# Alternating row halves in the small products, 32 bytes in front of the working memory, and a varied order of split matmuls in sixteen projections

## The chip, the core and the metric

The kernel runs on one core of a Trainium2 chip. A core has TensorE (PE, with its weight loads shown apart as PEld), VectorE (DVE), ScalarE (ACT), GpSimd (POOL) and SyncE (SP), which issues most DMAs. The metric is the device time of one execution in microseconds, lower is better. The kernel before takes 2512.82 us (median of three runs, 2508.73 to 2514.59).

## The reference

One layer of a hybrid decoder trunk over 256 tokens of width 2048, all in float32. The part that the change touches is the input projection and the RWKV-7 branch.

```python
def hybrid_mixer(h, positions, w_in, ...):
    z = h @ w_in
    z_sc, z_rw, z_ret, z_nsa, z_gate = _split(z, GROUP_SIZES)
    o_a = short_conv_mixer(*_split(z_sc, SC_SIZES), sc_conv)
    o_b = rwkv7_mixer(z_rw, ...)
    o_c = retention_mixer(*_split(z_ret, RET_SIZES), positions)
    o_d = nsa_mixer(*_split(z_nsa, NSA_SIZES), positions, ...)
    merged = g_a * (o_a @ w_a) + g_b * (o_b @ w_b) + g_c * (o_c @ w_c) + g_d * (o_d @ w_d)
    return merged @ w_out

def wkv7_scan(r, w, k, v, kk, a):          # inside rwkv7_mixer: 8 heads of 64 channels
    def step(state, inp):
        r_t, w_t, k_t, v_t, kk_t, a_t = inp
        sa = jnp.einsum('bhvk,bhk->bhv', state, -kk_t)
        state = (state * w_t[:, :, None, :]
                 + sa[..., None] * (kk_t * a_t)[:, :, None, :]
                 + v_t[..., None] * k_t[:, :, None, :])
        return state, jnp.einsum('bhvk,bhk->bhv', state, r_t)
    _, y = lax.scan(step, s0, xs)

def reference(...):
    x = x + rms_norm(hybrid_mixer(rms_norm(x, ...), ...), ...)
    x = x + rms_norm(memory_cross_attention(rms_norm(x, ...), rms_norm(mem, ...), ...), ...)
    x = x + rms_norm(conv_ffn(rms_norm(x, ...), ...), ...)
```

## The kernel before

Each engine runs a program of its own, written out by hand; semaphores alone tie them together. No scheduler moves anything: on each engine the instructions run as the code lists them.

**The stages.** First the normed input is made (until about 28 us). Then come the 79 tiles of the list `MIX`: one 1 MB weight tile each, multiplied with the 256 tokens, with the work of the four mixers laid between them by the table `steps`. From about 772 us the weights stream: gates and branches, output projection, cross-attention, and the feed-forward part up to the end. SP loads the weights of `MIX` into a ring of four slots.

**Two ways to multiply.** `project` (line 396) multiplies in plain float32. A plain float32 product shows as two records in the trace, each with its weight load, so that 16 products make 32 records. The first sixteen projections, `project_split` (lines 414 and 417), and the whole streaming part (`half`, lines 797 and 800) use a split form instead: a value is held as a rounded "high" part and a "low" rest. One product of 512 columns takes the high weights times the high and low activations side by side (`high`), and one of 256 columns the low weights times the high activations (`cross`); both go to one PSUM bank of 512 columns. Such a product is one record. ACT makes the high parts, DVE the low ones. The semaphore `hsplit_low` tells that a quarter of the activations is split; projection 0 waits for each quarter when it comes to it.

**The small products.** The RWKV-7 branch holds two heads of 64 channels in the two halves of the 128 partitions. Its products are 64 x 64 (some 64 x 128), read one half of the partitions and write the same half of PSUM, in the banks of `sm`. `per_head` (products at line 452) runs 32 of them: 16 for the lower half, then 16 for the upper half, each to a place of its own: eight 64-wide products fill a bank. It is called by `rw_s1` and `rw_s2` (128 wide), `rw_s3`, `rw_s4`, `rw_level` and `rw_level2` (64 wide). `four` (products at line 531) runs four products, or four sums of two or three, for each half in the same manner, for the four chunks `rw_chunk_a`, `rw_chunk_b`, `rw_chunk_c`. One projection lies between one such group and the next, while DVE or ACT evacuates the group's result and makes the operands of the next.

**The memory.** SBUF tensors are laid one behind another: the constants `cst`, the vectors `vec` (552 columns, 2208 bytes a partition), and `region`, in which all working tensors are placed by offset. `region` begins at byte 25632, which is 32 above a multiple of 64.

Of the kernel before, what the change touches and what calls it, by code (L numbers as in the profile page):

```python
# [19 lines left out]
T = 256  # L20
P = 128
# [84 lines left out]
NVEC = sum(c for _, c in VEC)  # L106
# [33 lines left out]
def program(nc, A, const_dram, decay_dram, const_at, out):  # L140
# [4 lines left out]
    with ctx:  # L145
        def sb(name, shape, dt=f32):
            return ctx.enter_context(nc.sbuf_tensor(name, shape, dt))
# [3 lines left out]
        def sem(name):  # L151
            if name not in sems:
                sems[name] = ctx.enter_context(nc.semaphore(name))
            return sems[name]

        NC = const_dram.shape[1]
        cst = sb("cst", [P, NC])
        vec = sb("vec", [P, NVEC])

        region_at = nc.sbuf_base  # L160
        sb("region", [P, REGION])
# [4 lines left out]
        def part(a, *dims, dt=f32):  # L166

            placed[0] += 1
            t = nc.alloc_sbuf_tensor_at(f"part{placed[0]}", [P, math.prod(dims)], dt, offset=region_at + 4 * a)
            names = "abcdef"[:len(dims)]  # L170
            return t[:, :].rearrange(f"p ({' '.join(names)}) -> p {' '.join(names)}", **dict(zip(names, dims)))

        def partr(a, *dims):

            return part(a, *dims, dt=mybir.dt.float32r)
# [20 lines left out]
        def vv(name, i=0, n=1, rows=P):  # L196
            a, _ = VEC_AT[name]
            return vec[0:rows, a + i:a + i + n]
# [8 lines left out]
        sm = ctx.enter_context(nc.psum_tensor("sm", [P, 6, 512], f32))  # L207
# [19 lines left out]
        hsplit = partr(A0 + 8208, KT, 2 * T)  # L227
# [48 lines left out]
        cross = part(21504, 2, T)  # L276
# [105 lines left out]
        def _(pe):  # L382
# [17 lines left out]
            def project_split(n):  # L400

                if n >= 2:
                    pe.wait_ge(outd, n - 1)
                b = bank[:, n % 2, :]
                for h in range(2):
                    pe.wait_ge(sem("early_low"), 2 * n + h + 1)
                    w = wearly[(2 * n + h) % 4]
                    for k in range(8):
                        if n == 0 and k % 4 == 0:
                            pe.wait_ge(sem("hsplit_low"), 2 * h + k // 4 + 1)  # L410
                        x, last = hsplit[:, 8 * h + k, :], h == 1 and k == 7
                        for term in ("cross", "high") if last else ("high", "cross"):
                            if term == "high":
                                mm = pe.matmul(b, w[:, 0, k, :], x, start=h == 0 and k == 0, stop=last,  # L414
                                               skip_group_check=True)
                            else:
                                mm = pe.matmul(b[:, T:2 * T], w[:, 1, k, :], x[:, 0:T], start=False, stop=False,  # L417
                                               skip_group_check=True)
                    mm.then_inc(sem("early_used"), 1)
                pe.sem_inc(used, 1)  # L420

# [16 lines left out]
            def per_head(fn):  # L438


                for h in range(2):
                    for g in range(16):
                        mm = fn(slice(64 * h, 64 * h + 64), g)
                return mm

            def b64(base, g, w=64):
# [42 lines left out]
            def rw_s1():  # L489
                pe.wait_ge(sem("rw_operands"), 1)  # L490
                pe.wait_ge(sem("rw_bonus_out"), 1)
                per_head(lambda r, g: small_mm(0, r, g, G["B"][r, g], QR[r, g, :, :], w=128)) \
                    .then_inc(sem("rw_s1_mm"), 1)

            def rw_s2():
                pe.wait_ge(sem("rw_s1_out"), 1)
                per_head(lambda r, g: small_mm(0, r, g, G["C"][r, g], QR[r, g, :, :], w=128)) \
                    .then_inc(sem("rw_s2_mm"), 1)

            def rw_s3():  # L500
                pe.wait_ge(sem("rw_s2_out"), 1)
                per_head(lambda r, g: small_mm(0, r, g, QR[r, g, 0, :], G["B"][r, g])).then_inc(sem("rw_s3_mm"), 1)
                per_head(lambda r, g: small_mm(2, r, g, G["Vc"][r, g], eye(r))).then_inc(sem("rw_s3_mm"), 1)
# [19 lines left out]
                        .then_inc(sem("rw_p2_mm"), 1)  # L523

            def four(base, off, fn):
                for h in range(2):
                    r = slice(64 * h, 64 * h + 64)
                    for i in range(4):
                        pairs = fn(r, i)
                        for q, (a, b) in enumerate(pairs):  # L530
                            mm = pe.matmul(sm[r, base + i // 2, off + i % 2 * 64:off + i % 2 * 64 + 64], a, b,  # L531
                                           start=q == 0, stop=q == len(pairs) - 1)
                return mm

            v4 = lambda a: a.rearrange("p (i t) -> p i t", t=64)
# [2 lines left out]
            def rw_chunk_a(c):  # L538

                if c == 0:  # L540
                    pe.wait_ge(sem("rw_x_ready"), 6)
                else:
                    pe.wait_ge(sem("rw_state"), c)
                    pe.wait_ge(sem("rw_y_out"), c)
                four(0, 0, lambda r, i: ([(QR[r, 4 * i + c, 0, :], S4[r, i])] if c else [])
                     + [(G["L2"][r, 4 * i + c], G["V"][r, 4 * i + c])]).then_inc(sem("rw_rhs_mm"), 1)

            def rw_chunk_b(c):

                pe.wait_ge(sem("rw_rhs_out"), c + 1)  # L550
                four(2, 0, lambda r, i: [(G["X"][r, 4 * i + c], X04[r, i])]).then_inc(sem("rw_u_mm"), 1)

            def rw_chunk_c(c):

                pe.wait_ge(sem("rw_u_out"), c + 1)
                if c < NCH - 1:
                    four(2, 128, lambda r, i: [(G["Bt"][r, 4 * i + c], U4[r, i]),
                                               (G["Ct"][r, 4 * i + c], G["V"][r, 4 * i + c])]) \
                        .then_inc(sem("rw_ds_mm"), 1)
                four(0, 128, lambda r, i: ([(S4[r, i], QR[r, 4 * i + c, 1, :])] if c else [])  # L560
                     + [(U4[r, i], G["M1"][r, 4 * i + c]), (G["V"][r, 4 * i + c], G["M2"][r, 4 * i + c])]) \
                    .then_inc(sem("rw_y_mm"), 1)
# [206 lines left out]
            for n, (what, i) in enumerate(MIX):  # L769
                for s in steps.get((what, i), []):  # L770
                    s()
                if n < EARLY:
                    project_split(n)
                elif what == "gate":
                    project(n, M=24)
                elif what == "cmp":
                    nsa_cmp_hidden(i)
                elif what == "rv":
                    take(n)
                    project_tokens(n, hT, big[:, n % 2, :])  # L780
                else:
                    project(n)
# [151 lines left out]
            with pe.Fori(0, 8) as i:  # L934
                for t in range(2):
                    pe.wait_ge(prod_out, i * 2 + (R_DOWN + t - 1))
                    for j in range(4):
                        if t == 0:
                            pe.wait_ge(sem("g_split"), 11 * j + 11)
                        for h, n in ((0, 8), (1, 3)):  # L940
                            k = 11 * j + 8 * h

                            x, k0 = (gA, k) if k < 8 else (gB, k - 8)
# [6 lines left out]
        def _(act):  # L950
            used, outd = sem("chunk_used"), sem("chunk_out")
            act.sem_inc(sem("prod_out"), 2)
            act.dma_start(cst[:, :], const_dram).then_inc(sem("consts_loaded"), 16)
            act.dma_start(vec[:, :], A["vec"]).then_inc(sem("consts_loaded"), 16)
            cp, idt = ACT.Copy, ACT.Identity

            def std(k):
# [312 lines left out]
            for j in range(KT):  # L1270
# [9 lines left out]
                elif 8 <= j < 12:  # L1280
                    q = j - 8
# [3 lines left out]
            for j in range(KT):  # L1285
# [3 lines left out]
                elif 2 <= j < 6:  # L1289
                    q = j - 2  # L1290
# [5 lines left out]
                elif 11 <= j < 15:  # L1296
                    q = j - 11
# [52 lines left out]
            for q in range(4):  # L1350
                act.wait_ge(sem("res_ready"), 4 + q + 1)
                for k in range(4 * q, 4 * q + 4):
                    mm = act.activation(yT[:, k, :], res[:, k, :], cp, scale=vv("ln_ffn_pre", k))
# [7 lines left out]
            for first, count, g in ((0, 8 // PAIR_STEP, gA), (4, (FT - 8) // PAIR_STEP, gB)):  # L1361
                with act.Fori(0, count) as i:
# [6 lines left out]
                    for p in range(PAIR_STEP):  # L1369
                        for s in range(2):  # L1370
                            j = 2 * p + s
                            m = M_UP + 4 * first + j
                            at = lambda k, v: i * (2 * PAIR_STEP * k) + v
# [776 lines left out]
```

## Time and profile before

| what | before |
|---|---|
| median of three timed runs | 2512.82 us |
| their range | 2508.73 to 2514.59 us |
| span of the profiled execution, first to last instruction | 2503.8 us |
| median of the runs less this span | 9.0 us |
| PE busy | 2398.1 us, 96% |
| weight loads on PE busy | 2085.0 us, 83% |
| DVE busy | 1384.9 us, 55% |
| ACT busy | 1045.6 us, 42% |
| POOL busy | 236.1 us, 9% |
| mean granted clock of PE | 0.975 of full speed |

The span comes from one profiled execution, and the last 9.0 us of a timed run lie around it. "Busy" counts a stretch once even where records overlap, so a group's busy time can be far less than its count times its mean duration. The granted clock is 1.00 where PE runs at 2.4 GHz and 0.50 where it runs at 1.2 GHz. A row of the timeline merges records of one kind that follow each other: its second number is the time from the first start to the last end.

### The profile page before, as it was taken

The numbers are of one execution on the slowest core, as the hardware profiler recorded it, in microseconds if no ns is written. First come the engines' busy times: TensorE is split into PE (matmuls) and PEld (weight loads), VectorE is DVE, ScalarE is ACT, GpSimd is POOL, SyncE is SP. The second block draws the span as 40 slices with busy tenths as digits, with TensorE's granted clock in tenths as the row PEclk, the third lists the DMA queues.
The fourth block names the chain that finished last, engine by engine and source line by source line (L and its number), as shares of the span: only waits on it lengthen the run. The fifth ranks groups of instructions, "written<-read, shape, count | busy, mean of one in ns | idle before, by whom it ended". The sixth has DMA issues, their size and how long they took to land.

```text
span 2503.8 us, 38637 instructions
## 1 busy us (share of the span) xinstructions
PE 2398.1 (96%) x14320; PEld 2085.0 (83%) x14320; DVE 1384.9 (55%) x1676; ACT 1045.6 (42%) x1463; POOL 236.1 (9%) x240
## 2 busy tenths in 40 slices
PE   5989999999999999999999999896999999999996
PEld 4869989789888888887887888785888888888885
DVE  5661110221118666666677544356877777776665
ACT  4320001112114555555444444345655555555553
POOL 0120100000000000000421000031111111111110
PEclk9989997999999999999999999998999999999998
DMA  6512222233334555556555554252655555555663
GB/s 224 185 51 85 98 102 78 97 133 113 124 118 152 185 187 186 189 189 212 194 171 165 181 173 153 93 188 86 198 186 186 184 182 188 189 163 188 186 185 127
DMA packets 104459, 392.77 MB, mean 157 GB/s; under 512 B 11600, under 2 KB 20048, under 8 KB 94000
## 3 DMA queue, kind: packets, MB, share of 16 engines
q1 hardware_dynamic: 104080, 390.31, 47.2%
q8 instruction: 67, 1.10, 0.2%
q10 hardware_dynamic: 288, 1.17, 0.1%
q14 instruction: 24, 0.20, 0.0%
HBM read 389.34 MB, written 2.10 MB: 156 GB/s over the span
## 4 chain that ended last, share of the span: by engine, by line
PE 73%; issue 18%; DVE 6%; ACT 1%; POOL 1%; DMA 0%; DVEq 0%; POOLq 0%; ACTq 0%
PE bank L797 29%; PE bank L800 15%; PE bank L396 13%; PE sm L452 3%; PE bank L414 2%; PE bank L426 2%; PE sm L531 1%; PE bank L417 1%; PE bank L615 1%; DVE part L1876 1%; DVE part L1970 1%; DVE part L1539 1%; PE sm L905 1%; PE sm L435 1%; PE sm L887 1%
## 5 line engine op out<-in xcount | busy, mean ns | idle before, releaser
L797 PE MATMUL bank<-part,part 128*128 128x512 f32 x4224 | 1488.4, 399 | 35.1 <-issue 16.3
L800 PE MATMUL bank<-part,part 128*128 128x256 f32 x4224 | 1150.6, 282 | 0.0
L1876 DVE TENSOR_TENSOR part<-part,part 128x1024 fp32r<-128x1024 f32 (+1 forms) x632 | 795.0, 1268 | 370.7 <-ACT part L1139 358.4
L797 PEld LDWEIGHTS bank<-part,part 128*128 128x128 f32 x4224 | 783.8, 189 | 212.0 <-issue 20.1
L800 PEld LDWEIGHTS bank<-part,part 128*128 128x128 f32 x4224 | 799.7, 189 | 21.5
L1139 ACT ACTIVATE part<-part 128x1024 fp32r<-128x1024 f32 (+1 forms) x632 | 662.8, 1050 | 349.7 <-PE bank L800 320.9
L396 PE MATMUL bank<-part,part 128*128 128x256 f32 (+1 forms) x1632 | 364.3, 383 | 0.0
L396 PEld LDWEIGHTS bank<-part,part 128*128 128x128 f32 (+1 forms) x1632 | 307.4, 190 | 50.0 <-issue 5.1
L1213 ACT ACTIVATE part<-bank 128x256 f32<-128x256 f32 x236 | 90.3, 382 | 291.1 <-PE bank L797 291.1
L992 ACT ACTIVATE part<-bank 128x256 f32<-128x256 f32 (+1 forms) x59 | 22.7, 384 | 413.3 <-PE bank L396 375.5
L1884 DVE TENSOR_TENSOR part<-bank,part 128x256 f32<-128x256 f32 (+1 forms) x236 | 99.8, 423 | 132.9 <-ACT part L1213 132.8
L1476 POOL TENSOR_TENSOR part<-part 128x256 f32 (+1 forms) x48 | 48.1, 1003 | 763.2 <-DVE part L1884 763.2
L797 PE MATMUL sm<-part,part 128*128 128x512 f32 x320 | 110.8, 397 | 1.3 <-DVE part L1890 0.7
L414 PE MATMUL bank<-part,part 128*128 128x512 f32 x256 | 90.9, 403 | 8.7 <-DVE part L1575 8.7
L800 PE MATMUL sm<-part,part 128*128 128x256 f32 x320 | 79.4, 281 | 0.0
L452 PEld LDWEIGHTS sm<-part 64*64 64x64 f32 x1088 | 71.6, 139 | 7.6 <-issue 7.6
L452 PE MATMUL sm<-part 64*64 64x64 f32 (+1 forms) x1088 | 73.7, 233 | 2.1 <-DVE part L1639 2.1
L1501 POOL TENSOR_TENSOR part<-part 128x256 f32<-128x256 f32 x44 | 32.5, 738 | 424.1 <-DVE part L2051 424.1
L417 PE MATMUL bank<-part,part 128*128 128x256 f32 x256 | 69.8, 283 | 0.0
L797 PEld LDWEIGHTS sm<-part,part 128*128 128x128 f32 x320 | 56.8, 188 | 11.0 <-DVE part L1890 1.5
L800 PEld LDWEIGHTS sm<-part,part 128*128 128x128 f32 x320 | 60.1, 188 | 5.8
L414 PEld LDWEIGHTS bank<-part,part 128*128 128x128 f32 x256 | 47.7, 190 | 20.4 <-issue 9.7
(304 smaller groups left out, 1576.0 us busy)
## 6 DMA issues: line engine op xcount, KB each, us to landing
part<-in_w_up SPq DMA_DIRECT2D x176, 512.0 KB, 4.5
part<-in_w_g SPq DMA_DIRECT2D x104, 512.0 KB, 4.2
part<-in_w_dn SPq DMA_DIRECT2D x64, 512.0 KB, 3.5
part<-in_w_out SPq DMA_DIRECT2D x32, 512.0 KB, 4.0
part<-in_w_mk SPq DMA_DIRECT2D x32, 512.0 KB, 4.3
part<-in_w_mv SPq DMA_DIRECT2D x32, 512.0 KB, 3.9
part<-in_w_q SPq DMA_DIRECT2D x32, 512.0 KB, 3.8
part<-in_w_o SPq DMA_DIRECT2D x32, 512.0 KB, 3.9
```

Of the source, the lines that this page charges most:

```text
L396: mm = pe.matmul(big[0:M, n % 2, 0:rhs_n], w[:, k * M:(k + 1) * M], x[:, k, :], start=k == 0, stop=k == KT - 1)
L414: mm = pe.matmul(b, w[:, 0, k, :], x, start=h == 0 and k == 0, stop=last, skip_group_check=True)
L417: mm = pe.matmul(b[:, T:2 * T], w[:, 1, k, :], x[:, 0:T], start=False, stop=False, skip_group_check=True)
L426: mm = pe.matmul(dst[:, s * P:(s + 1) * P], x[:, k, s * P:(s + 1) * P], ring[:, n % NSLOT, k, :], start=k == 0, stop=k == KT - 1)
L452: return pe.matmul(sm[rows, b, c:c + w], lhsT, rhs, start=start, stop=stop)
L797: mm = pe.matmul(dst, w[:, 0, k, :], x[:, k0 + k, :], start=start and k == 0, stop=last, skip_group_check=True)
L800: mm = pe.matmul(dst[:, T:2 * T], w[:, 1, k, :], x[:, k0 + k, 0:T], start=False, stop=False, skip_group_check=True)
L1139: act.activation(wsplit[(2 * m + h) % 4][:, 0, 0:n, :], raw[:, m % 2, h, 0:n, :], cp) .then_inc(sem("hi_done"), 1)
L1213: act.activation(cross[:, b, :], bank[:, b, T:2 * T], cp).then_inc(sem("cross_out"), 1)
L1476: pool.tensor_tensor(sq[:, n % 2:n % 2 + 1, :], tile, tile, MUL).then_inc(sem("y_sq"), 1)
L1876: tt(w[:, 1, 0:n, :], raw[:, m % 2, h, 0:n, :], w[:, 0, 0:n, :].bitcast(f32), SUB).then_inc(sem("lo_done"), 1)
L1884: tt(dst, bank[:, b:b + 1, 0:T], cross[:, b:b + 1, :], ADD).then_inc(sem("prod_out"), 1)
```

## The change

Three things are edited.

First, `per_head` and `four` issue for the lower and the upper half in turn, and the upper half is shifted by half of the places, so that the two neighbours write different PSUM banks. Second, `vec` gets 8 more columns that nothing reads: `region`, `rstd` and `small` move up by 32 bytes, and `region` then begins at byte 25664, a multiple of 64. Third, `project_split` varies the order of its products. The second half of each projection runs backwards. Projections 1, 5, 9 and 13 run eight `high` and then eight `cross` products. Projections 2, 6, 10 and 14 issue each `high` product as two of 256 columns with the same weights. For projection 0 the second half of the weights waits for the last quarter of the activations at once.

```diff
-        vec = sb("vec", [P, NVEC])
+        vec = sb("vec", [P, NVEC + 8])
@@ project_split
-                    for k in range(8):
-                        if n == 0 and k % 4 == 0:
-                            pe.wait_ge(sem("hsplit_low"), 2 * h + k // 4 + 1)
-                        x, last = hsplit[:, 8 * h + k, :], h == 1 and k == 7
-                        for term in ("cross", "high") if last else ("high", "cross"):
-                            if term == "high":
-                                mm = pe.matmul(b, w[:, 0, k, :], x, start=h == 0 and k == 0, stop=last,
-                                               skip_group_check=True)
-                            else:
-                                mm = pe.matmul(b[:, T:2 * T], w[:, 1, k, :], x[:, 0:T], start=False, stop=False,
-                                               skip_group_check=True)
+                    grouped, halves = n % 4 == 1, n % 4 == 2
+                    terms = [("high", k) for k in range(8)] + [("cross", k) for k in range(8)] if grouped else \
+                        [(term, k) for k in range(8) for term in ("high", "cross")]
+                    if h == 1:
+                        terms = terms[::-1]
+                    for at, (term, k) in enumerate(terms):
+                        if n == 0 and at % 8 == 0:
+                            pe.wait_ge(sem("hsplit_low"), 2 * h + at // 8 + 1 if h == 0 else 4)
+                        x, last = hsplit[:, 8 * h + k, :], h == 1 and at == 15
+                        first = h == 0 and at == 0
+                        if term == "cross":
+                            mm = pe.matmul(b[:, T:2 * T], w[:, 1, k, :], x[:, 0:T], start=False, stop=last,
+                                           skip_group_check=True)
+                        elif halves:
+                            pe.matmul(b[:, 0:T], w[:, 0, k, :], x[:, 0:T], start=first, stop=False,
+                                      skip_group_check=True)
+                            mm = pe.matmul(b[:, T:2 * T], w[:, 0, k, :], x[:, T:2 * T], start=False, stop=last,
+                                           skip_group_check=True)
+                        else:
+                            mm = pe.matmul(b, w[:, 0, k, :], x, start=first, stop=last, skip_group_check=True)
@@ per_head
-                for h in range(2):
-                    for g in range(16):
-                        mm = fn(slice(64 * h, 64 * h + 64), g)
+                for g in range(16):
+                    for h in range(2):
+                        mm = fn(slice(64 * h, 64 * h + 64), (g + 8 * h) % 16)
@@ four
-                for h in range(2):
-                    r = slice(64 * h, 64 * h + 64)
-                    for i in range(4):
-                        pairs = fn(r, i)
-                        for q, (a, b) in enumerate(pairs):
-                            mm = pe.matmul(sm[r, base + i // 2, off + i % 2 * 64:off + i % 2 * 64 + 64], a, b,
-                                           start=q == 0, stop=q == len(pairs) - 1)
+                rows = [slice(64 * h, 64 * h + 64) for h in range(2)]
+                for i in range(4):
+                    at = [(i + 2 * h) % 4 for h in range(2)]
+                    pairs = [fn(rows[h], at[h]) for h in range(2)]
+                    for q in range(len(pairs[0])):
+                        for h in range(2):
+                            a, b = pairs[h][q]
+                            c = off + at[h] % 2 * 64
+                            mm = pe.matmul(sm[rows[h], base + at[h] // 2, c:c + 64], a, b,
+                                           start=q == 0, stop=q == len(pairs[h]) - 1)
@@ scalar
-            act.dma_start(vec[:, :], A["vec"]).then_inc(sem("consts_loaded"), 16)
+            act.dma_start(vec[:, 0:NVEC], A["vec"]).then_inc(sem("consts_loaded"), 16)
```

PE, projection 0, as its second half of the weights (`part_63`) begins; before, it reads:

```order
L417 MATMUL bank<-part_61,part_62 128x256
L414 MATMUL bank<-part_61,part_63 128x512 [waits hsplit_low,early_low]
L417 MATMUL bank<-part_61,part_63 128x256
L414 MATMUL bank<-part_61,part_63 128x512
L417 MATMUL bank<-part_61,part_63 128x256
```

PE at the same place in the changed kernel (line 414 has become 427, line 417 has become 419):

```order
L419 MATMUL bank<-part_61,part_62 128x256
L419 MATMUL bank<-part_61,part_63 128x256 [waits hsplit_low,early_low]
L427 MATMUL bank<-part_61,part_63 128x512
L419 MATMUL bank<-part_61,part_63 128x256
L427 MATMUL bank<-part_61,part_63 128x512
```

The half begins with a `cross` product, and its wait for `hsplit_low` is now for all four quarters and no longer for three.

PE in a projection with halved `high` products (lines 422 and 424), changed kernel, as one half of the weights ends and the next begins:

```order
L422 MATMUL bank<-part_61,part_62 128x256
L424 MATMUL bank<-part_61,part_62 128x256
L419 MATMUL bank<-part_61,part_62 128x256
L419 MATMUL bank<-part_61,part_63 128x256 [waits early_low]
L422 MATMUL bank<-part_61,part_63 128x256
```

Three products of 256 columns stand where one of 512 and one of 256 stood, which is 16 more products in each of the four projections. In `per_head` and `four` the number of products, their shapes and their waits stay; only which half each one works on changes, and the rows of such a list don't name the half. The lists of SP, DVE, ACT and POOL hold the same instructions in the same order.

## Rows read from the trace of the kernel before

**Rows 1.** The page: PE's busy time; costliest group, with count, busy us, mean ns.

```profile
PE 2398.1 (96%) x14320; PEld 2085.0 (83%) x14320; DVE 1384.9 (55%) x1676; ACT 1045.6 (42%) x1463; POOL 236.1 (9%) x240
...
L797 PE MATMUL bank<-part,part 128*128 128x512 f32 x4224 | 1488.4, 399 | 35.1 <-issue 16.3
```

**Rows 2.** Waits, 120 to 200 us: who waited for whom, us, times, longest.

```profile
PE sm L486 <- DVE part L1632: 7.6, 1, 7.6
...
PE sm L463 <- ACT part L996: 3.8, 1, 3.8
```

**Rows 3.** Windows: length, busy us and records by engine, granted clock, DMA share, GB/s.

```profile
175.00:180.00 5.00, 5.00 (x29) 5.00 (x29) 0.00 (x0) 0.00 (x0) 0.00 (x0) 0.50 0.01 3
...
200.00:250.00 50.00, 50.00 (x554) 45.65 (x553) 7.35 (x6) 3.58 (x6) 5.58 (x7) 1.00 0.23 85
```

**Rows 4.** Groups by shape on PE, 160 to 480 us: busy us, mean ns.

```profile
L452 PE MATMUL sm<-part 64*64 64x64 f32 x960 | 54.9, 220 | 0.0
L531 PE MATMUL sm<-part 64*64 64x64 f32 x448 | 31.4, 251 | 0.0
...
L452 PE MATMUL sm<-cst,part 64*64 64x64 f32 x192 | 10.9, 220 | 0.0
```

**Rows 5.** Timeline of PE, 200 to 210 us: start, length, engine, line, records.

```profile
208.00 0.27 PE L452 MATMUL sm<-cst,part 64*64 64x64 f32 x1
208.05 0.22 PE L452 MATMUL sm<-part 64*64 64x64 f32 x1
208.10 0.22 PE L452 MATMUL sm<-cst,part 64*64 64x64 f32 x1
208.11 0.22 PE L452 MATMUL sm<-part 64*64 64x64 f32 x1
208.16 0.22 PE L452 MATMUL sm<-cst,part 64*64 64x64 f32 x1
```

**Rows 6.** Timeline of PE, 170 to 480 us: groups of small products, one projection.

```profile
170.33 11.98 PE L452 MATMUL sm<-part 64*64 64x128 f32 x64 [2.10 <-DVE part L1639]
...
190.77 6.82 PE L452 MATMUL sm<-part 64*64 64x128 f32 x64
197.52 7.17 PE L396 MATMUL bank<-part,part 128*128 128x256 f32 x32
...
218.79 7.14 PE L452 MATMUL sm<-cst,part 64*64 64x64 f32 x128
...
232.96 3.76 PE L452 MATMUL sm<-part 64*64 64x64 f32 x64
...
356.16 0.96 PE L531 MATMUL sm<-part 64*64 64x64 f32 x16
...
371.07 5.99 PE L531 MATMUL sm<-part 64*64 64x64 f32 x64
...
387.07 1.90 PE L531 MATMUL sm<-part 64*64 64x64 f32 x32
...
400.48 7.70 PE L531 MATMUL sm<-part 64*64 64x64 f32 x80
...
435.31 4.34 PE L531 MATMUL sm<-part 64*64 64x64 f32 x80
...
469.68 2.83 PE L531 MATMUL sm<-part 64*64 64x64 f32 x48
```

**Rows 7.** Timeline of DVE and of PE, 32 to 37 us: the first projection.

```profile
32.74 2.36 DVE L1575 TENSOR_TENSOR part<-part,part 128x1024 fp32r<-128x1024 f32 x2
...
34.12 0.47 PE L414 MATMUL bank<-part,part 128*128 128x512 f32 x1 [1.10 <-DVE part L1575]
34.42 0.28 PE L417 MATMUL bank<-part,part 128*128 128x256 f32 x1
...
34.77 0.28 PE L417 MATMUL bank<-part,part 128*128 128x256 f32 x1
...
36.50 0.39 PE L417 MATMUL bank<-part,part 128*128 128x256 f32 x2
```

## The prediction, made before the changed kernel was run

> **What bounds the kernel now.** I read the page first: PE is busy in 96% of the span, and every other engine in 55% or less [rows 1]. So the question for each edit is what it does to PE's own time, and where PE waits for others. The chain of waits between 120 and 200 us shows where it does: 3.8 us for ACT, at the end of a chain from DVE, and 7.6 us for DVE, in the stretch that prepares the RWKV-7 operands [rows 2]. That chain starts when the sixteen early projections end, so whatever delays them delays everything. From 200 us on PE has no idle time: the window from 200 to 250 us has 50.00 us busy of 50.00, with DVE busy 7.35 us, ACT 3.58 and the DMAs at 23% [rows 3]. What PE saves there is saved at the end, as long as the engines between two groups keep up.
>
> Then the small products. The groups by shape show three large ones of 64-wide products, 54.9, 10.9 and 31.4 us busy [rows 4]; two groups of 128-wide ones add 11.98 and 6.82 us [rows 6]. That is 116 us in which a quarter of the array works at a time. The timeline gives their pace: 128 records in 7.14 us, 0.056 us each [rows 6]. The most telling rows stand where one call of `per_head` ends and another begins, at 208 us [rows 5]. There the end of the first call (upper half, `part`) and the start of the second (lower half, `cst`) run together: starts at 208.00, 208.05, 208.10, 208.11, 208.16. The `cst` records start 0.10 and then 0.06 us apart, the `part` records 0.05 to 0.06 apart, each at its usual pace. Two halves side by side don't slow each other. They overlap only for the last three records of the old half, at each change of half.
>
> **The small products in turn.** If every product has a neighbour in the other half, all records can run as these six do. The step of one half is then 7.14 us less a tail of 0.22, over 127 steps less the 9 that the three changes of half already hide: 0.0586 us. A group of n records takes about 0.10 (first step) + (n/2 - 2) x 0.0586 + 0.22 (tail). From [rows 6], with the number of such groups that the timeline has:
>
> - 128 records: 7.14 us become 3.95, saved 3.2. Six of them: 19.1 us.
> - 64 records: 3.76 become 2.08, saved 1.7. Six: 10.1 us.
> - `four`, full clock: 16 records 0.96 become 0.67 (five groups, 1.4 us saved); 32 records 1.90 become 1.14 (three, 2.3 us); 80 records 4.34 become 2.55 (1.8 us); 48 records 2.83 become 1.61 (1.2 us).
> - `four` at a granted clock of 0.5, where the step is twice as long, about 0.107 us: 5.99 us become 3.7 (saved 2.3), 7.70 become 4.5 (saved 3.2).
> - 128-wide (`rw_s2`): 64 records in 6.82 us, step 0.109; 3.7 us after, saved 3.1. `rw_s1` takes 11.98 us because it runs mostly at 1.2 GHz (0.50 granted from 175 to 180 us, [rows 3]). Ten pairs at 0.109 and 22 at twice that are some 6.1 us, saved 5.8.
>
> Sum 50.3 us. Is there cover for the others? Between two groups lies one projection of 7.17 us [rows 6]. Its length doesn't change, and in it DVE or ACT makes the next operands: at most three DVE operations of the size that takes 1.2 us [rows 7]. DVE's 7.35 us and the DMAs' 23% in 50 us [rows 3] leave room for a pace a quarter faster. I cost new waits at nothing; should the cover be gone in one step, that costs 1 to 2 us.
>
> Here a rule of the Trainium skill can be set beside the rows. "TensorE: Matmul & The Clock Gate", Part 3, says that a weight load overlaps a running matmul only where the row group differs, which is what the alternation makes, and that matmuls start strictly in program order. By [rows 5] the trace disagrees with the second: a `cst` record starts at 208.00, ahead of three `part` records that stand before it in the program. The sum is the same by either.
>
> **The first sixteen projections.** In projection 0 the second half of the weights started at 34.12 us, right after the third quarter was split; two such DVE operations run from 32.74 for 2.36 us [rows 7]. Waiting for the fourth moves it to about 35.2, by 1.1 us. PE then catches up with nothing, since it is busy without a gap until the last early projection. Halved products: a `high` and a `cross` product together take 0.35 us (34.42 to 34.77), and two of 256 columns in a row are 0.39 - 0.28 = 0.11 to 0.12 us apart [rows 7]. Three of 0.12 are 0.36, so 0.006 us more for each of 64: 0.4 us. An upper bound, a whole 0.12 us for each additional product, would be 7.7 us. Grouping and running backwards change no count: nothing. Sum: 1.5 us lost.
>
> **The 32 bytes.** No row of before shows `region` at another alignment. Below: the pair of 512 and 256 columns takes 0.35 us, where 768 columns at 2.4 GHz would be 0.32; if the 0.03 us went away in each of the 4224 pairs [rows 1], that were 127 us gained. Above: the same lost. Against both: the loss looks like a share of the columns (0.12 for 256, 0.235 for 512), not like a fixed cost at the start of a row, and a shift of the start should touch only the latter. I take nothing, the middle. "SBUF — State Buffer" (Door 1) of the Trainium skill gives lines of 16 bytes, and a shift by 32 leaves the place within such a line as it was; no row here shows that.
>
> **Sum.** 2503.8 - 50.3 + 1.5 = 2455.0 us of span. The median of the runs lies 9.0 us above that span, so 2464 us.
>
> **The rivals.**
>
> *PE can't be fed two records in 0.058 us (10%).* The six records of [rows 5] may have come from a queue that was filled while the old half ran. If records come in at no more than one in 0.056 us, nothing is saved and 1.5 us are lost: 2514 us. In between, say at one in 0.04 us, the 64-wide groups at full clock (65.4 us in `per_head`, 17.7 in `four`) save 28%, 23 us, and the 128-wide ones and those at the low clock their whole 14.4: 2477 us; at 0.05, 2488. I give the between 7% and no saving 3%. For it: no row shows such a pace for long. Against it: two starts within 0.01 us, and after them no pause. "TensorE: Matmul & The Clock Gate" of the Trainium skill says that without hardware decoding a matmul costs about 62 ns of the sequencer, by which nothing would be saved; steps of 0.056 us [rows 6] are already below that, so the trace disagrees.
>
> *Each change of half costs the long first step (4%).* The second half to start needs 0.10 us to its second record instead of 0.06 [rows 5]. If that is the price of every change and not of a fresh start, each small product pays 0.16 us instead of 0.112. For 576 + 224 + 64 products that is some 41 us more: 2555 us, slower. It decides if less than a quarter of the records find a running neighbour. Against it: the old half kept its 0.055 while the new one started.
>
> *The 32 bytes matter (10%).* Mostly as a gain, since a multiple of 64 is the more natural place: half of the 127 us with the rest as forecast gives 2400 us, all of it 2337. A loss (2% of the 10) of the same kind: 2500 to 2540 us.
>
> *The clock falls elsewhere (within the forecast).* In projection 0 the gap before the second half grows from 1.1 to 2.2 us; if the clock falls to 1.2 GHz after it, 2 us more. The low stretches in which the groups at 371.07 and 400.48 us run [rows 6] may shrink or move with the denser work: 5 us either way. `rw_s1` ends 6 us earlier, and its projection may start at the low clock, 1 to 2 us.
>
> **How the numbers follow.** The forecast, full overlap and no effect of the 32 bytes, has 74%, with a range of its own of 2452 to 2476 us: 12 us below for low stretches that shrink and the same above for steps a tenth longer or a wait that comes up. The other 2% is a wait that takes back most of the saving: near 2500. To leave out no more than 2 in 10 the range goes from 2448 to 2490 and takes in the slower feed; it leaves out the 32 bytes at either side and the two rivals without a saving. About 0.2%, 5 us, is what can be told from no change. Faster has 74 + 7 + 8 + 2 = 91%; same the 3% of no saving; slower 4 + 2 = 6%.
>
> **What would show it.** In the profile after: the groups at line 452, now 461, 128 records in about 3.9 us and 64 in 2.1; busy time at the former lines 452 and 531 down from 116 us to about 66; PE still without idle time from 200 us on; the second half of projection 0 starting at about 35.2 us; pairs in the streaming part still 0.35 us apart. Rows with small records 0.056 us apart would mean that PE isn't fed; steps of 0.10, that changing halves costs; pairs of 0.33 or 0.37 us in the streaming part, that the alignment matters. What would make the prediction wrong is above all that last one, since it multiplies by 4224.

## The result and the profile after

The changed kernel took 2455.18 us (median of 4 runs, 2451.77 to 2458.48), the kernel before 2510.78 us (4 runs, 2508.73 to 2514.59): a ratio of 0.9776, with a 95% interval of 0.9761 to 0.9792. The profiled execution has a span of 2450.0 us against 2503.8, so 53.8 us less; forecast were 48.8.

The 9.0 us between median and span before don't lie around the span, as I had taken them to. In every execution on record that lists both, the time is 1.7 to 1.8 us above its own span (2451.77 and 2450.0 for the profiled one of the changed kernel). The rest of the 9.0 is that the profiled execution was faster than the median of the timed ones.

The page of the changed kernel, with PE's busy time and its costliest group, beside [rows 1] (line 797 is now 809):

```profile
PE 2345.9 (96%) x14384; PEld 2035.3 (83%) x14384; DVE 1383.9 (56%) x1676; ACT 1045.3 (43%) x1463; POOL 236.6 (10%) x240
...
L809 PE MATMUL bank<-part,part 128*128 128x512 f32 x4224 | 1489.3, 400 | 36.0 <-issue 16.3
```

PE's busy time falls by 52.2 us; that of the 4224 large streaming products and of the other engines stays. The groups by shape of the changed kernel, PE, 160 to 425 us, beside [rows 4] (`per_head` is line 461 now, `four` 543):

```profile
L461 PE MATMUL sm<-part 64*64 64x64 f32 x960 | 30.4, 219 | 0.0
L543 PE MATMUL sm<-part 64*64 64x64 f32 x448 | 18.9, 247 | 0.0
L461 PE MATMUL sm<-part 64*64 64x128 f32 x128 | 9.2, 309 | 1.8 <-DVE part L1651 1.8
...
L461 PE MATMUL sm<-cst,part 64*64 64x64 f32 x192 | 6.0, 219 | 0.0
```

The reader is to see two numbers that move apart. The mean of one record stays (219 ns after, 220 before), so no product became faster. The busy time, in which what overlaps counts once, falls from 54.9 to 30.4 us, and over all small products from 116.0 to 64.5. Two products now stream where one streamed.

Could it be instead that only the weight load of one half is now hidden behind the product of the other? The step between records settles it. With the same 64x64 weights, the step on one half is 0.0586 us for 64 columns and 0.109 us for 128 (the prediction's reading of [rows 6]). So nearly all of a step, by estimate 0.05 of the 0.0586 us, grows with the columns, and a weight load that can't be hidden would be at most the 0.01 us that is left. After the change a record starts every 0.031 us, which is less than the columns of one take: the columns of two products stream at the same time.

The timeline shows the single groups, and also what comes between them. PE, changed kernel, 160 to 430 us, beside [rows 6]:

```profile
170.52 5.47 PE L461 MATMUL sm<-part 64*64 64x128 f32 x64 [1.84 <-DVE part L1651]
175.93 7.17 PE L396 MATMUL bank<-part,part 128*128 128x256 f32 x32
183.03 3.71 PE L461 MATMUL sm<-part 64*64 64x128 f32 x64
...
204.76 3.95 PE L461 MATMUL sm<-cst,part 64*64 64x64 f32 x128
...
215.74 2.08 PE L461 MATMUL sm<-part 64*64 64x64 f32 x64
...
329.71 2.08 PE L543 MATMUL sm<-part 64*64 64x64 f32 x64
331.72 4.44 PE L627 MATMUL bank<-part,part 128*128 128x30 f32 x32
...
353.52 4.54 PE L543 MATMUL sm<-part 64*64 64x64 f32 x80
...
383.28 2.55 PE L543 MATMUL sm<-part 64*64 64x64 f32 x80
...
414.83 1.61 PE L543 MATMUL sm<-part 64*64 64x64 f32 x48
416.38 7.17 PE L396 MATMUL bank<-part,part 128*128 128x256 f32 x32
```

In the brackets of the first row stands the only wait of these rows. From 200 to 430 us PE waits once, 0.47 us for ACT, as it did before: no small product and no projection behind one comes late. Windows of the changed kernel, 200 to 300 us and 320 to 420 us (length, busy time and records of PE, PEld, DVE, ACT, POOL, granted clock, DMA share, GB/s), beside [rows 3]:

```profile
200.00:300.00 100.00, 100.00 (x1280) 88.31 (x1279) 19.35 (x30) 4.87 (x11) 16.77 (x21) 1.00 0.30 106
320.00:420.00 100.00, 99.53 (x845) 84.50 (x845) 14.57 (x39) 13.93 (x33) 0.76 (x2) 0.88 0.31 109
```

### The profile page after: what moved, and what is told of

It is laid out like the page before. It is cut to its first block, busy times and chain, and to the rows that moved or that the text cites. A ratio compares the mean times of both kernels' runs of the same rounds, so it can differ in the third digit from the quotient of the medians.

```text
span 2450.0 us, 38765 instructions
## 1 busy us (share of the span) xinstructions
PE 2345.9 (96%) x14384; PEld 2035.3 (83%) x14384; DVE 1383.9 (56%) x1676; ACT 1045.3 (43%) x1463; POOL 236.6 (10%) x240
## 4 chain that ended last, share of the span: by engine, by line
PE 73%; issue 19%; DVE 6%; ACT 1%; POOL 1%; DMA 0%; DVEq 0%; POOLq 0%; ACTq 0%
PE bank L809 30%; PE bank L812 15%; PE bank L396 13%; PE bank L435 2%; PE sm L461 2%; PE bank L427 2%; PE bank L419 1%; DVE part L1888 1%; PE bank L627 1%; PE sm L543 1%; DVE part L1982 1%; PE sm L917 1%; DVE part L1551 1%; PE sm L444 1%; PE sm L899 1%
## 5 line engine op out<-in xcount | busy, mean ns | idle before, releaser
L809 PE MATMUL bank<-part,part 128*128 128x512 f32 x4224 | 1489.3, 400 | 36.0 <-issue 16.3
L427 PE MATMUL bank<-part,part 128*128 128x512 f32 x192 | 63.1, 407 | 7.6 <-DVE part L1587 7.6
L1398 ACT ACTIVATE part<-part,vec 128x256 f32<-128x256 f32 x88 | 52.5, 597 | 17.6 <-DVE part L2057 13.2
L1491 POOL TENSOR_TENSOR part<-part,part 128x256 f32<-128x256 f32 x48 | 58.5, 1220 | 6.3 <-POOL part L1488 5.1
```

The lines of the kernel that those rows point to most:

```text
L427: mm = pe.matmul(b, w[:, 0, k, :], x, start=first, stop=last, skip_group_check=True)
L809: mm = pe.matmul(dst, w[:, 0, k, :], x[:, k0 + k, :], start=start and k == 0, stop=last, skip_group_check=True)
L1398: act.activation(ub[:, p % 2, s, :], rawu[:, s, :], ACT.Identity, bias=col(b0), scale=col(w2)) \
L1491: pool.tensor_tensor(acc.unsqueeze(1), acc.unsqueeze(1), sq[:, n % 2:n % 2 + 1, :], ADD).then_inc(sem("y_acc"), 1)
```

## The experiments

Each ratio is against the kernel before, measured on the same chip in the same round of runs. The rounds ran on different chips, so ratios are compared and not times.

**The edits one by one.** The theory: all of the gain comes from overlap between halves; the 32 bytes and the new order of the early projections do next to nothing. The rival: one of them matters, and the total only hides it. The first kernel has `per_head` and `four` of the change and all else from before.

```diff
@@ per_head (and four, as in the change)
-                for h in range(2):
-                    for g in range(16):
-                        mm = fn(slice(64 * h, 64 * h + 64), g)
+                for g in range(16):
+                    for h in range(2):
+                        mm = fn(slice(64 * h, 64 * h + 64), (g + 8 * h) % 16)
```

> Only per_head and four of the change (halves in turn, upper half shifted by half of the places). My theory: all of the gain is here, so the span falls by 53 to 57 us against before, ratio 0.977 to 0.979, and the whole change is within 2 us of it. Rival, that the 32 bytes or the order of the split products give part of the gain: this kernel gains clearly less, under 50 us.

Measured: 2451.45 us, ratio 0.9772 (0.9759 to 0.9786). That is the whole gain of the change. Of span, 53 to 57 us less was expected. The profiled execution, with 2455.1 us, is only 48.7 us shorter, but it was the slowest of five; the median one has 2449.7 us.

The second has only the 8 columns more in `vec`:

```diff
-        vec = sb("vec", [P, NVEC])
+        vec = sb("vec", [P, NVEC + 8])
...
-            act.dma_start(vec[:, :], A["vec"]).then_inc(sem("consts_loaded"), 16)
+            act.dma_start(vec[:, 0:NVEC], A["vec"]).then_inc(sem("consts_loaded"), 16)
```

> Only the 8 unused columns behind vec, so that all working tensors lie 32 bytes higher. My theory: nothing, ratio 0.999 to 1.001, and the pair of split products in the streaming part stays at 0.352 us. Rival, that the place of an operand within 64 bytes matters to TensorE's reads: a pair pace other than 0.352 by 0.001 us or more, which 4224 pairs make 4 us or more.

Measured: 2509.19 us, ratio 1.0003 (0.9994 to 1.0012). The windows of this kernel and of the changed one, PE alone, show the same number of records in the same 600 us of the streaming part. First the kernel with the 32 bytes alone:

```profile
1800.00:2400.00 600.00, 600.00 (x3397) 1.00 0.57 185
```

Then the changed kernel:

```profile
1800.00:2400.00 600.00, 600.00 (x3398) 1.00 0.56 184
```

The kernel before has 3397 there too, so that a pair takes 0.353 us in all three. This agrees with "SBUF — State Buffer" (Door 1) of the Trainium skill, which gives lines of 16 bytes: a shift by 32 bytes leaves the place within a line as it was.

The third has only the new `project_split`:

```diff
@@ project_split
-                    for k in range(8):
...
+                    grouped, halves = n % 4 == 1, n % 4 == 2
...
+                    if h == 1:
+                        terms = terms[::-1]
```

> Only the new order of the products in project_split. My theory: the last of the sixteen early projections ends 1.0 to 1.5 us later (the wait for the last quarter, and 64 halved products at 0.007 us), and most of it is lost in the wait for VectorE that follows: span 0 to 1.5 us longer, ratio 1.000 to 1.001. Rival, that the delay passes on whole and the clock falls longer after it: 1.5 to 4 us longer, 1.001 to 1.002.

Measured: 2509.32 us, ratio 1.0007 (0.9997 to 1.0016). The interval holds both nothing and the 1.5 us (0.06%) that I had counted as lost; it excludes the 7.7 us of the upper bound. It doesn't exclude the rival, 1.5 to 4 us.

The last has only `per_head` of the change, with `four` as before:

> Only per_head in turn, four as before. By the terms of my sum per_head saves 29.2 us in the 64-wide groups and 8.9 in the 128-wide ones, so 38 us and up to 2 more from a clock that rises sooner after the first group: span 36 to 41 us under before, ratio 0.984 to 0.986. Rival, that the extra gain over the sum (5 us) comes from the first groups rather than from four and the low clock around it: 43 us or more.

Measured: 2467.24 us, ratio 0.9845 (0.9828 to 0.9861), so 38.9 us; the span is 40.2 us shorter, where 36 to 41 was expected. `four` has the rest.

**Must the two halves write different banks?** The change also shifts the places of the upper half, so that neighbours never write one PSUM bank. A rival to pure overlap of halves was that this shift is what makes it possible. This kernel takes turns without the shift, so that each pair writes one bank, on different partitions:

```diff
-                        mm = fn(slice(64 * h, 64 * h + 64), (g + 8 * h) % 16)
+                        mm = fn(slice(64 * h, 64 * h + 64), g)
...
-                    at = [(i + 2 * h) % 4 for h in range(2)]
+                    at = [i for h in range(2)]
```

> Halves in turn as in the change, but without the shift of the upper half by half of the places: both neighbours write the same PSUM bank, on different partitions. Theory A, that the overlap comes from the two halves of the array alone: as the first run of this call, 0.977 to 0.979. Theory B, that two products that run at once can't write one bank: the small products keep their step of about 0.056 us a record, no gain, ratio 0.999 to 1.001, or a longer step and slower than before.

Measured: 2449.85 us, ratio 0.9772 (0.9757 to 0.9787), the same as with the shift. The timeline of PE in this kernel:

```profile
204.00 3.95 PE L452 MATMUL sm<-cst,part 64*64 64x64 f32 x128
...
214.98 2.08 PE L452 MATMUL sm<-part 64*64 64x64 f32 x64
```

3.95 and 2.08 us, to the hundredth as in the changed kernel. "TensorEngine Tiling (Array Packing)" of the Trainium skill, Restrictions and Gotchas, says that different row tiles can't access one PSUM bank at the same time; for these 64x64 products on two halves the trace disagrees.

**How far ahead of its turn does the other half start?** [rows 5] showed the new half starting ahead of the last three records of the old one. Theory: a record of the idle half starts once no more than three records of the running half wait ahead of it (each product is two records). Runs of two products are then nearly as good as turns. Rival: only strict alternation is fast, and each change of half costs. The three kernels below change `per_head` alone, and switch the half every two, four or eight products (`four` in turn as in the change):

```diff
-                for g in range(16):
-                    for h in range(2):
-                        mm = fn(slice(64 * h, 64 * h + 64), (g + 8 * h) % 16)
+                for g0 in range(0, 16, 2):          # 4 and 8 in the others
+                    for h in range(2):
+                        for g in range(g0, g0 + 2):
+                            mm = fn(slice(64 * h, 64 * h + 64), (g + 8 * h) % 16)
```

> The halves in turn, but in per_head in runs of two products (four records) a half; four as in the change. My theory, read from the rows at 208 us of before: TensorE picks a record of the other half when no more than three of the running half still wait ahead of it. A run of four records never hides the other half, so 64 records take 2.1 us and 128 records 3.95 us, as with runs of one. Rival, strict pairing: only direct neighbours run together, one of two records of a run has a partner, and 64 records take 2.9 us or more.

> The same in runs of four products (eight records). Theory of three waiting records: the other half starts when the fifth of eight records starts, loses one step at its own start, and each run costs five steps of 0.058 in place of four: 64 records take 2.4 to 2.7 us. Rival, a long window (a whole queue of records looked through): 2.1 us as in turn. Strict pairing: 3.5 us or more.

> The same in runs of eight products (sixteen records, two changes of half more than before has in 64 records). Theory of three waiting records: three records saved at each of three changes, 64 records take 3.76 - 2 x 3 x 0.058 = 3.4 us. Long window: about 2.1 to 2.6 us. Strict pairing: 3.6 us or more.

Timeline of PE with a switch every two products:

```profile
204.47 4.00 PE L453 MATMUL sm<-cst,part 64*64 64x64 f32 x128
...
215.50 2.13 PE L453 MATMUL sm<-part 64*64 64x64 f32 x64
```

Every four:

```profile
206.65 4.99 PE L453 MATMUL sm<-cst,part 64*64 64x64 f32 x128
...
218.67 2.69 PE L453 MATMUL sm<-part 64*64 64x64 f32 x64
```

Every eight:

```profile
216.30 6.42 PE L453 MATMUL sm<-cst,part 64*64 64x64 f32 x128
...
229.76 3.40 PE L453 MATMUL sm<-part 64*64 64x64 f32 x64
```

| switch every | 64 records, us | ratio (95%) |
|---|---|---|
| 1 product, the change's own two edits | 2.08 | 0.9772 (0.9759 to 0.9786) |
| 2 | 2.13 | 0.9767 (0.9747 to 0.9786) |
| 4 | 2.69 | 0.9804 (0.978 to 0.9829) |
| 8 | 3.40 | 0.9882 (0.9863 to 0.9902) |
| 16 (before) | 3.76 | 1 |

The ratios for 2, 4 and 8 rest on two timed runs each. The two for 4 lie 10 us apart (2453.93 and 2464.0 us), so the middle column carries the argument.

Runs of two cost next to nothing (0.05 us a group); that speaks for the theory and against a price per change of half. In runs of four and eight the overlap gets rarer; by the theory, the other half can't start until few enough records wait ahead of it. With three records 2.4 to 2.7 us were expected for runs of four and 3.4 for runs of eight; 2.69 and 3.40 came out. The depth of three is inferred from these times and from the rows where `part` gives way to `cst`, which show three records left in the kernels with runs of four and eight too; it wasn't varied by itself.

**Does the clock explain the rest?** The span fell by 5.0 us more than my sum. The theory: less time of the NSA stretch lies at the low clock, and how much does so depends on where the small and the 30-column products lie. So I spread them: four `cmp` projections that stood in a row are now mixed with the `q` ones, with the steps between them kept at their places. Once with small products in turn, and once on the kernel before:

```diff
-        + [("sc", i) for i in range(12)] + [("kv", i) for i in range(6)] + [("cmp", i) for i in range(4)]
-        + [("q", i) for i in range(4)] + [("gate", 0)]
+        + [("sc", i) for i in range(12)] + [("kv", i) for i in range(6)]
+        + [("cmp", 0), ("q", 0), ("cmp", 1), ("q", 1), ("cmp", 2), ("cmp", 3), ("q", 2), ("q", 3), ("gate", 0)]
```

> The halves in turn as in the first run, and the list MIX in another order around 320 us: cmp 0, q 0, cmp 1, q 1, cmp 2, cmp 3, q 2, q 3, the work of steps left at the same places of the list. So full projections lie between products of 30 columns. Theory: what differs from run to run by some 5 us beyond my sum is the time at the low clock in this stretch (15 to 25 us of it, half of which is lost); apart, the low stretch shrinks below 10 us, and the span is 3 to 8 us shorter than with the halves in turn alone (2445 us), less 1 to 2 us for a new wait, since the output of cmp 3 is wanted right after it. Rival: the low clock falls anyway after the small products, and the time is that of the halves in turn alone or 1 to 2 us more.

> The same order of MIX on the kernel before. Theory of the low clock: before has 34 us at the low clock between 369 and 411 us, of which this takes at least half away: 6 to 12 us faster, 0.995 to 0.998. Rival: with the long small products of before the clock falls anyway, nothing or 1 to 2 us slower.

Measured, in turn: 2445.81 us, ratio 0.9754 (0.974 to 0.9767), the fastest kernel of the study, 5.6 us below the same without the mix. The two intervals overlap, so that by the times alone these 5.6 us are likely, not settled. The wait that I had expected with them didn't come. Its window (columns as above):

```profile
320.00:420.00 100.00, 99.53 (x861) 84.18 (x860) 14.57 (x39) 13.91 (x33) 0.75 (x2) 0.91 0.32 114
```

And that of the kernel with the two edits alone, unmixed:

```profile
320.00:425.00 105.00, 104.53 (x847) 89.39 (x846) 14.56 (x39) 13.94 (x33) 0.75 (x2) 0.84 0.30 107
```

With the granted clock either 1 or 0.5, a mean of 0.91 over 100 us is 2 x 0.09 x 100 = 18 us at the low level, and 0.84 over 105 us is 34. So the direction was right, though I had expected under 10 us.

On the kernel before the mix gave 2505.89 us, ratio 0.9989 (0.998 to 0.9998), where 0.995 to 0.998 was expected: a miss. In its profiled execution there is about as much time at the low level as without it (a mean of 0.82 over the 112 us from 360 us on, some 40 us, against 37 before). The mix alone doesn't hold the clock up.

These windows are of one execution each, and that of the unmixed kernel was its slowest. But every timed run lists its span and its mean granted clock, and span x (1 - clock) is an estimate of what the low level cost it: half of the time spent there.

| kernel, runs | mean span, us | mean clock | cost of the low level, us | span less this cost, us |
|---|---|---|---|---|
| before, 15 | 2506.2 | 0.9743 | 64.5 | 2441.8 |
| before, mixed, 11 | 2503.7 | 0.9752 | 62.1 | 2441.5 |
| in turn, 5 | 2450.0 | 0.9786 | 52.4 | 2397.6 |
| in turn, mixed, 5 | 2444.4 | 0.9810 | 46.4 | 2397.9 |
| the whole change, 4 | 2453.4 | 0.9768 | 57.0 | 2396.3 |

The clock is on record to 0.001, which is 2.5 us, so the table is good to a microsecond or so. The last column doesn't move with the mix; what the mix gains, 5.6 and 2.5 us of mean span, is all in the clock (6.0 and 2.4 us). So the theory holds for the gain of the mix. The last row also shows why the whole change took a few microseconds longer than the halves in turn alone: its runs had the lower clock. Of the 56.2 us between the first row and the third, 12 are clock; a part of them is in the forecast, through the small products that had run at the low level.

## Why the prediction came out right

The mechanism was right and carries nearly all of the gain. On medians the change gained 55.6 us (2510.78 - 2455.18) where 48.8 was forecast. Most of the difference is a clock term that I had named but left at nothing, and that it fell on the good side was luck.

**The mechanism.** The pace per half was right: 3.95 and 2.08 us were forecast for 128 and 64 records, 3.95 and 2.08 came out. The six records of [rows 5] could be carried to all 1728 small records (960 + 448 + 128 + 192). The rivals of a slow feed (0.04 us and more a record) and of a long first step at each change fall by the same rows: 128 records in 3.95 us are one in 0.031 us, at every change of half. (In the first of these rivals, a feed of one record in 0.05 us gives 2491 us by the prediction's own terms, not 2488; nothing rests on it. And the 62 ns that it sets against steps of 0.056 us are stated for a case without hardware decoding; no trace here shows whether this is that case, so the steps don't speak against that figure.)

Two sentences need a limit. "No scheduler moves anything" holds for the lists, but on TensorE a record can start ahead of some that are listed before it [rows 5]. And "from 200 us on PE has no idle time" holds for the window it was read from, not for the rest: the waits from 200 us to the end add up to 49 us before and 50 after. They stayed nearly the same, and so the saved time did reach the end.

**The terms.** The small products were to save 50.3 us and saved 51.5 (116.0 to 64.5).

- The twelve `per_head` groups of 64-wide products: forecast 29.2 us; 54.9 + 10.9 became 30.4 + 6.0, so 29.4.
- `rw_s2`: forecast 3.7 us, measured 3.71. `rw_s1`: forecast 6.1, measured 5.47. I had counted more of it at the low clock than then ran there (0.50 granted until 174 us, 0.96 from 174 to 176).
- `four`: the 80-record groups were forecast at 2.55 and 4.5 us and took 2.55 and 4.54. The 64-record group was forecast at 3.7 for a low clock and took 2.08, because the clock was up when it came (1.00 granted from 329.7 to 331.7 us). One group of 32 and one of 16 records went the other way: 1.93 and 1.12 us, forecast at 1.14 and 0.67. In the kernel with the two edits alone the very same group ran at the low clock (0.50 granted). Its timeline of PE:

```profile
331.01 3.68 PE L534 MATMUL sm<-part 64*64 64x64 f32 x64
```

**The early projections: mis-sized.** I had 1.5 us lost. In projection 0 the second half now starts at 35.01 us instead of 34.12. Timeline of PE, changed kernel, 32 to 37.7 us, beside [rows 7]:

```profile
33.45 0.41 PE L419 MATMUL bank<-part,part 128*128 128x256 f32 x1
35.01 0.36 PE L419 MATMUL bank<-part,part 128*128 128x256 f32 x1 [1.14 <-DVE part L1587]
35.20 0.39 PE L427 MATMUL bank<-part,part 128*128 128x512 f32 x1
```

The last early product starts at 122.44 us against 121.44: 1.0 us late. But the first group of small products starts at 170.52 us against 170.33, so only 0.2 of it is left there. Between the two PE waits for DVE; the waits of the changed kernel, 120 to 200 us, beside [rows 2]:

```profile
PE sm L495 <- DVE part L1644: 5.4, 1, 5.4
PE sm L472 <- ACT part L1008: 3.8, 1, 3.8
PE sm L461 <- DVE part L1651: 1.8, 1, 1.8
```

The wait of 7.6 us is now 5.4: PE came to it 2.6 us later than before (the products after the 3.8 us wait ran slower, too: line 472, eight records, 3.75 us against 2.32), while DVE's work came only 0.4 us later, and at the next wait 0.2. So my sentence that whatever delays the early projections delays everything was wrong in these two profiles: PE's delay goes into its waits for DVE. How much is left at the end is not settled. In the profile with the new order alone the first group starts at 170.96 us, in the one with the small products in turn alone at 170.06, so that 0.2 us lies within the scatter between executions.

Where a `high` product is halved, three products take 0.36 us from start to start, and the pair elsewhere 0.353: 0.007 us for each of the 64, as forecast (0.006). PE, changed kernel, 46.8 to 49.1 us, a first row and the one six steps later:

```profile
46.84 0.28 PE L422 MATMUL bank<-part,part 128*128 128x256 f32 x1
...
49.00 0.28 PE L422 MATMUL bank<-part,part 128*128 128x256 f32 x1
```

**What I had left out.** The same stretch of the program, from the end of DVE's chain to the projection behind the last small product, is 472.44 - 170.33 = 302.1 us before and 416.38 - 170.52 = 245.9 after: 56.2 us less, and the small products are 51.5 of it. The rest is in products that nobody touched. Groups by shape of the kernel before, PE, 160 to 472 us:

```profile
L396 PE MATMUL bank<-part,part 128*128 128x256 f32 x640 | 146.6, 388 | 0.0
...
L615 PE MATMUL bank<-part,part 128*128 128x30 f32 x128 | 22.3, 344 | 0.0
```

And of the changed kernel, 160 to 416 us:

```profile
L396 PE MATMUL bank<-part,part 128*128 128x256 f32 x640 | 144.9, 385 | 0.0
...
L627 PE MATMUL bank<-part,part 128*128 128x30 f32 x128 | 19.3, 315 | 0.0
```

3.0 us in the 30-column products and 1.7 us in the projections: the clock is at its low level for less time. I had named this as "5 us either way" and left it out of the sum; it came out at the favourable end. It isn't owed to the change in any firm way: the kernel with the two edits alone has the same sequence of products there, and spends about 34 us at the low level in that stretch, against 24 (a mean of 0.88 over 100 us) in the changed one. Its span is 2455.1 us, where the changed kernel has 2450.0; their medians over several executions, 2451.45 and 2455.18, stand the other way round. The timed runs say the same: over five of them the kernel with the two edits alone shows a mean clock between 0.977 and 0.980, and its slowest run is the one with 0.977. So the split is luck as much as design, and what decides where in this stretch the clock falls stays open.

**What was given back.** By the first streaming product the changed kernel is ahead by 772.25 - 716.18 = 56.1 us, at the end by 53.8. Of the 2.3 us that are lost after it, 1.1 are in one wait of the streaming part that grew from 1.4 to 2.5 us (PE, line 809, for DVE, line 1915). The other 1.2 us I haven't traced.

**The median.** Of the 8.8 us by which 2464 was too high, 5.0 are the span's; the other 3.8 come from taking the 9.0 us between median and span as fixed. It was 5.2 us in the changed kernel, of which 1.8 lie around the span; the rest is by how much the profiled execution beat the median. That is scatter between executions, and taking it as fixed was the mistake.

## What to carry to other kernels

Products that fill half the rows and half the columns of the array, here plain float32 ones of 64 x 64 that write the half they read, should alternate between the halves in program order, in runs of at most two: that took away nearly half of their time, with no other cost, and a shift to different PSUM banks wasn't needed. To price it, look for a place where one half ends and the other begins, and see in the single records whether both keep their pace. When an early stage gets late, look where its chain of waits ends before you count the delay through.

## What the runs showed of the hardware

- TensorE starts records out of program order when the half of the array that they need is idle [rows 5]. The times fit a look of about three waiting records ahead: 64 records took 2.08, 2.13, 2.69, 3.40 and 3.76 us with runs of 1, 2, 4, 8 and 16 products.
- The two halves write one PSUM bank at once, on different partitions, without cost (ratio 0.9772 and 3.95 us for 128 records, with and without sharing).
- On one half, a plain float32 record of 64 columns steps 0.0586 us and one of 128 columns 0.109, with the same weights; on both halves together a record comes every 0.031 us.
- The stretch with 30-column and small products spends 18 to 37 us at the low clock in kernels that differ little (0.91 over 100 us in one; 0.83 over 107.7 us, from 364.7 us on, before). On a change worth 5 us, that would hide the result of a single execution. Span x (1 - mean clock), over all timed runs, takes this part out.
